# Expert weights stored piece by piece in HBM, an early dummy silu per expert, and result rows added by half rows, in a two-layer trunk kernel

## What is computed

```python
def expert_block(args):
    xb, e = args
    return (jax.nn.silu(xb @ w_gate[e]) * (xb @ w_up[e])) @ w_down[e]
...
y = ys[dest] * g_sorted[:, None].astype(h.dtype)
out = jnp.zeros((T, D), h.dtype).at[tok_sorted].add(y)
```

## Time and profile before

| | us |
|---|---|
| median of three runs | 1378.86 |
| the profiled execution | 1379.58 |
| its span in the trace | 1377.8 |
| PE busy | 1349.4 |
| DVE busy | 1111.5 |
| ACT busy | 920.1 |

### The profile page before, as it was taken

How to read it: one execution, slowest core, us unless ns; L and a number is a source line. 1 busy time by engine, 2 the same in 40 slices (tenths; PEclk the granted TensorE clock), 3 DMA queues, 4 the chain that set the end, 5 groups by cost and what they waited for, 6 DMA issues and landing times.

```text
span 1377.8 us, 17441 instructions
## 1 busy us (share of the span) xinstructions
PE 1349.4 (98%) x6369; PEld 1120.4 (81%) x6369; DVE 1111.5 (81%) x811; ACT 920.1 (67%) x747; POOL 33.8 (2%) x48
## 2 busy tenths in 40 slices
PE   9999999999999999999999999999999999999997
PEld 7888888787877887888788788888878888888775
DVE  5756666655678888888988888898888889889987
ACT  6554444445647777777777777777777777777674
POOL 0000000000110000000000000000000000002000
PEclk9999999999989999999999999999999999999999
DMA  9666775462339999999999999999999999999992
GB/s 347 218 206 181 216 214 191 163 204 92 113 125 372 374 378 362 394 372 364 392 372 370 369 391 372 370 383 366 384 367 392 369 368 388 373 377 381 394 362 93
DMA packets 194940, 431.27 MB, mean 313 GB/s; under 512 B 19601, under 2 KB 22033, under 8 KB 194897
## 3 DMA queue, kind: packets, MB, share of 16 engines
q1 hardware_dynamic: 178752, 415.66, 82.8%
q0 software_dynamic: 3360, 11.78, 2.2%
q10 hardware_dynamic: 12784, 3.26, 1.7%
HBM read 424.89 MB, written 5.78 MB: 313 GB/s over the span
## 4 chain that ended last, share of the span: by engine, by line
PE 89%; DVE 5%; ACT 3%; issue 2%; DMA 0%; ACTq 0%; POOL 0%; DVEq 0%
PE bank_G L1248 10%; PE bank_G L1250 10%; PE bank_G L1249 10%; PE bank_U L1248 9%; PE bank_U L1250 9%; PE bank_U L1249 9%; PE bank_Y L1248 8%; PE bank_Y L1250 8%; PE bank_Y L1249 8%; DVE w_lo L752 2%; PE bank_T L1689 2%; ACT w_hi L454 1%; PE bank_T L1248 1%; PE bank_T L1250 1%; PE bank_T L1249 1%
## 5 line engine op out<-in xcount | busy, mean ns | idle before, releaser
L752 DVE TENSOR_TENSOR w_lo<-raw,w_hi 128x2048 fp32r<-128x2048 f32 x390 | 885.8, 2289 | 195.2 <-ACT w_hi L454 195.1
L454 ACT ACTIVATE w_hi<-raw 128x2048 fp32r<-128x2048 f32 x390 | 747.0, 1919 | 286.7 <-PE bank_U L1250 91.1
L1248 PE MATMUL bank_Y<-w_hi,hidT_hi 128*128 128x512 f32 x492 | 192.3, 391 | 0.0
L1250 PE MATMUL bank_Y<-w_hi,hidT_lo 128*128 128x512 f32 x492 | 191.6, 390 | 0.0
L1249 PE MATMUL bank_Y<-w_lo,hidT_hi 128*128 128x512 f32 x492 | 191.5, 389 | 0.0
L1248 PE MATMUL bank_G<-w_hi,xg_hi 128*128 128x512 f32 x448 | 175.6, 392 | 11.0 <-DVE w_lo L752 10.0
L1248 PE MATMUL bank_U<-w_hi,xg_hi 128*128 128x512 f32 x448 | 179.1, 400 | 0.0
L1250 PE MATMUL bank_U<-w_hi,xg_lo 128*128 128x512 f32 x448 | 175.0, 391 | 0.0
L1250 PE MATMUL bank_G<-w_hi,xg_lo 128*128 128x512 f32 x448 | 174.5, 390 | 0.0
L1249 PE MATMUL bank_U<-w_lo,xg_hi 128*128 128x512 f32 x448 | 174.5, 390 | 0.0
L1249 PE MATMUL bank_G<-w_lo,xg_hi 128*128 128x512 f32 x448 | 174.4, 389 | 0.0
(11 more groups left out here) (302 smaller groups left out, 1366.6 us busy)
## 6 DMA issues: line engine op xcount, KB each, us to landing
raw<-in_expert_w_gate SPq DMA_DIRECT2D x112, 1024.0 KB, 7.4
raw<-in_expert_w_up SPq DMA_DIRECT2D x112, 1024.0 KB, 7.5
raw<-in_expert_w_down SPq DMA_DIRECT2D x112, 1024.0 KB, 7.4
raw<-in_nat_w_qkv SPq DMA_DIRECT2D x12, 1024.0 KB, 5.1
raw<-in_ffn_w_gate SPq DMA_DIRECT2D x11, 1024.0 KB, 8.9
raw<-in_ffn_w_up SPq DMA_DIRECT2D x11, 1024.0 KB, 6.0
raw<-in_ffn_w_down SPq DMA_DIRECT2D x11, 1024.0 KB, 5.1
raw<-in_fourier_w_out SPq DMA_DIRECT2D x4, 1024.0 KB, 15.9
```

The lines of the kernel that those rows point to most:

```text
L454: nc.scalar.activation(w_hi[w][:], raw[s][:], ACT.Copy).then_inc(hi_made, 1)
L752: nc.vector.tensor_tensor(w_lo[w][:], raw[s][:], w_hi[w][:].bitcast(f32), ALU.subtract).then_inc(lo_made, 1)
L1248: nc.tensor.matmul(out_, xh, wh, start=start, stop=False)
L1250: return nc.tensor.matmul(out_, xl, wh, start=False, stop=stop)
```

## The change

Three things. The experts' weights are rearranged on the host into an array of 336 pieces of 128 x 2048, so that each partition of a piece is one run of 8192 bytes. On ACT every expert begins with a silu of one column (which nothing reads), and the splitting of piece 3 goes from the end of the expert before to entry 0 of its own expert, on ACT and DVE. The adding of fetched rows is cut into eight instructions of 128 x 512 in place of four of 128 x 1024, two in each of four steps. (In the second sweep, which is not entered, waits and splits are moved to match.)

```diff
-def expert_source(ewg, ewu, ewd, e, j):
-
-    kind, c, half = EXPERT[j]
-    v = {"gate": ewg, "up": ewu, "down": ewd}[kind][0].rearrange("e (k p) n -> p (e k) n", p=P)
-    if kind == "down":
-        return v[:, bass.ds(e * (FFE // P) + (BANK // P * c + KROW * half), KROW), :], KROW, D
-    return v[:, bass.ds(e * KD + KH * half, KH), BANK * c:BANK * (c + 1)], KH, BANK
+def expert_source(expert_w, e, j):
+
+    return expert_w[bass.ds(e * PER_EXPERT + j, 1)].rearrange("a p n -> p (a n)"), 1, PIECE
...
         def expert(E, ahead, kept=True):
 
+            nc.scalar.activation(mo["silu_first"][:], half_power[:, 0:1], ACT.Silu)
             for j, (kind, c, half) in enumerate(EXPERT):
-                if j < AHEAD - SPLIT:
-                    continue
...
                 if ahead or j + SPLIT < PER_EXPERT:
                     split_hi(j + SPLIT, E)
-            if ahead:
-                for j in range(PER_EXPERT + SPLIT, PER_EXPERT + AHEAD):
-                    split_hi(j, E)
 
         gather_hi(1)
         assert made[0] == N1
-        for j in range(SPLIT, AHEAD):
-            split_hi(j, 0)
...
-        def add_terms(n):
-
-            for b in range(NB):
-                dve.wait_ge(s_terms, 16 * 2 * NB)
-                if n:
-                    dve.wait_ge(terms_added, b + 1)
-                nc.vector.scalar_tensor_tensor(out=h[:, b], in0=mo[("hn_hi", "hn_lo")[n]][:, b].bitcast(f32),
-                                               scalar=mo[("g1", "g2")[n]][:, b:b + 1], in1=h[:, b],
-                                               op0=ALU.mult, op1=ALU.add).then_inc(terms_added, 1)
+        def add_term(n, b, q):
+
+            cs = slice(BANK * q, BANK * (q + 1))
+            dve.wait_ge(s_terms, 16 * 2 * NB)
+            if n:
+                dve.wait_ge(terms_added, 2 * b + q + 1)
+            nc.vector.scalar_tensor_tensor(out=h[:, b, cs], in0=mo[("hn_hi", "hn_lo")[n]][:, b, cs].bitcast(f32),
+                                           scalar=mo[("g1", "g2")[n]][:, b:b + 1], in1=h[:, b, cs],
+                                           op0=ALU.mult, op1=ALU.add).then_inc(terms_added, 1)
...
-                    elif c == 2:
-                        add_terms(0)
-                    elif c == 3:
-                        add_terms(1)
+                    elif 2 <= c < 6:
+                        add_term((c - 2) // 2, c % 2, 0)
...
+                if (kind, half) == ("down", 0) and kept and not sweep and 1 <= c < 5:
+                    add_term((c - 1) // 2, (c - 1) % 2, 1)
...
+def laid_out(w, k0, tiles, c0, width):
+
+    return w.reshape(-1, P, w.shape[-1])[k0:k0 + tiles, :, c0:c0 + width].transpose(1, 0, 2).reshape(P, PIECE)
+
+
+def experts_by_piece(inputs):
+
+    laid = np.empty((NE * PER_EXPERT, P, PIECE), np.float32)
+    for e in range(NE):
+        for j, (kind, c, half) in enumerate(EXPERT):
+            w = np.asarray(inputs[f"expert_w_{kind}"][0][e])
+            place = (BANK // P * c + KROW * half, KROW, 0, D) if kind == "down" else (KH * half, KH, BANK * c, BANK)
+            laid[PER_EXPERT * e + j] = laid_out(w, *place)
+    return laid
```

More of the change, by code:

```diff
@@ L114 @@
 NO_RESULT = (NE - 1) * P
-def expert_source(ewg, ewu, ewd, e, j):
-    kind, c, half = EXPERT[j]
-    v = {"gate": ewg, "up": ewu, "down": ewd}[kind][0].rearrange("e (k p) n -> p (e k) n", p=P)
-    if kind == "down":
-        return v[:, bass.ds(e * (FFE // P) + (BANK // P * c + KROW * half), KROW), :], KROW, D
-    return v[:, bass.ds(e * KD + KH * half, KH), BANK * c:BANK * (c + 1)], KH, BANK
+def expert_source(expert_w, e, j):
+    return expert_w[bass.ds(e * PER_EXPERT + j, 1)].rearrange("a p n -> p (a n)"), 1, PIECE
 def trunk(nc, x, norm_mix, norm_ffn, w_in, w_out, w_qkv, w_o, ffg, ffu, ffd, router_w, router_b,
-          ewg, ewu, ewd, final_norm, gains_c, slide_c, dft_c, mask_c, ident_c, before_c, count_c, out):
+          final_norm, expert_w, gains_c, slide_c, dft_c, mask_c, ident_c, before_c, count_c, out):
     f32, f32r, bf16, i32, u32 = mybir.dt.float32, mybir.dt.float32r, mybir.dt.bfloat16, mybir.dt.int32, mybir.dt.uint32
@@ L134, in trunk @@
     N0 = len(dense)
-    dense += [expert_source(ewg, ewu, ewd, 0, j) for j in range(SPLIT)]
+    dense += [expert_source(expert_w, 0, j) for j in range(SPLIT)]
     N1 = len(dense)
@@ L202, in trunk @@
     arena_start = nc.sbuf_base
-    mo_more = [("y_row", [P, D], f32), ("place", [P, 2, NB], f32), ("past", [P, 2, NB], f32), ("source", [P, 2, NB], u32)]
+    mo_more = [("y_row", [P, D], f32), ("place", [P, 2, NB], f32), ("past", [P, 2, NB], f32), ("source", [P, 2, NB], u32), ("silu_first", [P, 1], f32)]
     moe_l += mo_more
@@ L360, in own_loads @@
             for j in range(AHEAD, PER_EXPERT):
-                src, tiles, _ = expert_source(ewg, ewu, ewd, E % NE, j)
+                src, tiles, _ = expert_source(expert_w, E % NE, j)
                 load(j, E, src, tiles)
@@ L366, in next_loads @@
             for j in range(PER_EXPERT, PER_EXPERT + AHEAD):
-                src, tiles, _ = expert_source(ewg, ewu, ewd, (E + 1) % NE, j % PER_EXPERT)
+                src, tiles, _ = expert_source(expert_w, (E + 1) % NE, j % PER_EXPERT)
                 load(j, E, src, tiles)
         for j in range(SPLIT, AHEAD):
-            src, tiles, _ = expert_source(ewg, ewu, ewd, 0, j)
+            src, tiles, _ = expert_source(expert_w, 0, j)
             load(j, 0, src, tiles)
@@ L726, in _ @@
             act.wait_ge(hn_made, NB)
-            act.wait_ge(terms_added, 2 * NB)
+            act.wait_ge(terms_added, 4 * NB)
             for b in range(NB):
@@ L730, in _ @@
             gather_hi(NE + 1)
-            for j in range(PER_EXPERT, PER_EXPERT + AHEAD):
+            for j in range(PER_EXPERT, PER_EXPERT + SPLIT):
                 split_hi(j, LAST)
@@ L734, in _ @@
                 expert(E, True)
+            split_hi(PER_EXPERT + SPLIT, SECOND[1] - 1)
             act.wait_ge(e_added, NB * (NE + 1))
@@ L1110, in add_result @@
             for b in range(NB):
-                dve.wait_ge(terms_added, NB + b + 1)
+                dve.wait_ge(terms_added, 4 * NB)
                 for q in range(2):
@@ L1785 @@
 _INS = ["x", "norm_mix", "norm_ffn", "fourier_w_in", "fourier_w_out", "nat_w_qkv", "nat_w_o",
-        "ffn_w_gate", "ffn_w_up", "ffn_w_down", "router_w", "router_b", "expert_w_gate", "expert_w_up",
-        "expert_w_down", "final_norm"]
+        "ffn_w_gate", "ffn_w_up", "ffn_w_down", "router_w", "router_b", "final_norm"]
 _OUTS = [((1, S, D), "float32")]
@@ L1818 @@
     gains = np.stack([inputs["norm_mix"], inputs["norm_ffn"]], 1).reshape(4, KD, P).transpose(2, 0, 1)
-    for name, a in [(n, inputs[n]) for n in _INS] + [("gains", gains), ("slide", slide)] + list(shape_constants().items()):
+    for name, a in [(n, inputs[n]) for n in _INS] + [("expert", experts_by_piece(inputs)), ("gains", gains), ("slide", slide)] + list(shape_constants().items()):
         a = np.ascontiguousarray(a)
```

## The result

The changed kernel takes 1368.84 us (median of four runs, 1367.73 to 1369.60) against 1378.80 before: a ratio of 0.9928, 95% interval 0.9911 to 0.9945. The forecast was 1368.0 us, range 1366.8 to 1372.0.

The account below looks back on a forecast made before the run. PE, busy 98% of the span, bounds the kernel, so only its stalls can yield time. Profiled 1379.58 - 8.3 (silu) + 0.3 (piece 3) - 2.9 (half rows), layout 0, = 1368.7; 0.72 above median, so 1368.0 us, range 1366.8 to 1372.0.

Parts of the forecast that it names:

- Silu's table early: Experts 0 to 6: loading silu's table before piece 3's copy removes PE's wait at piece 4, 8.3 us gained.
- Rival 3: ACT in the loop: compiler keeps a load ahead of the real silu too, fourteen loads, 1376.3 us or more; chance 0.03.
- Piece 3 on DVE: Expert 7: result_places comes ahead of piece 3's split on DVE, so PE starts late, 0.3 us lost.
- Half rows: Expert 7, steps 2 to 5: adding by halves cuts PE's stalls of 3.7 us to 0.8, 2.9 us gained.
- rival 2: Expert 7's additions: half rows bring nothing, the eight together stalling as long as the four did, 1370.9 us; chance 0.10.
- The layout: Expert weight transfers: already hidden, so the longer runs are worth 0 on the path.
- rival 4: Weight transfers: 8192-byte runs move slower and become the bound; at 360 GB/s about +43 us, 1422 us; chance 0.04.
- The sum: Whole kernel: profiled 1379.58 - 8.3 + 0.3 - 2.9 = 1368.7, hence 1368.0 us for the median.

Follow-up runs that it names:

- second series: The changed kernel timed once more, unaltered, beside the kernel before and other follow-up kernels: 1367.78 us.
- spread kernel: Changed kernel with each half-row addition ahead of another split and six operations of gate_weights cut into three and three: 1366.85 us; with the old weight layout 1366.12 us.

## Why the prediction was right, and where it was not

- **Silu's table early**, 8.3 us: measured 8.6 alone, and 8.1 to 8.4 by the traces. The steps held to a tenth: the copy of piece 3 is 0.63 late (it starts 3.35 us after that of piece 2, where it was 2.72) for a forecast of 0.62, and 0.35 us are spare for a forecast of 0.33. PE stalls at no piece of the loop. Rival 3 fell: there are seven loads and not fourteen.
- **Piece 3 on DVE**, -0.3 us: this step was wrong, and so are two statements of the section on the change (that the splitting moves on ACT and DVE, and that DVE's `expert` loses the same lines as ACT's). The diff changes ACT alone; DVE had always taken piece 3 at the end of the expert before, and still does, which gives the same order of splits. The term is 0. The kernel that does move it lost 0.25 us, so the price was right for a change that wasn't made.
- **Half rows**, 2.9 us: 3.5 alone (interval 1.9 to 4.4) and 2.8 by the trace. Steps 2 to 5 take 16.9 to 17.0 us each against 16.8 undisturbed: the 0.2 forecast for each, so rival 2 fell. Where the 0.2 goes was partly luck. The prediction had the first half just fit and put all of it at the second gate piece. In the trace most of it is at the first: PE is due at 1280.22, starts at 1280.24 and then restarts slowly, so that the second gate piece starts at 1283.09, 2.85 us later in place of 2.72; the second piece adds about 0.08.

```profile
1279.99 0.39 PE L1241 MATMUL bank_Y<-w_hi,hidT_lo 128*128 128x512 f32 x1
1280.24 0.47 PE L1239 MATMUL bank_G<-w_hi,xg_hi 128*128 128x512 f32 x1
```

A start 0.02 us late costs 0.15 here, and one 0.13 late cost 0.25 when piece 3 was moved on DVE: most of the price of so small a stall is the restart.

- **The layout**, 0: right for the path, since faster transfers meet no one who waits for them; rival 4 fell the other way, with 421 GB/s in place of 402. Missed was the 0.5 to 0.6 us at the end, where the last store lands later; it has nothing to do with the runs.
- **The sum.** The trace's two middle parts give -11.2, the end +0.5, hence -10.7; the medians gave -10.0 and, in the second series, -10.3. That the forecast came within 0.9 us of the median owes something to luck: 0.3 us for a move that wasn't made stood where 0.5 at the end was missing. The 0.4 to 0.7 us that are left were not pinned down, but they are no more than the scatter of a stretch that the prediction took as fixed, the one ahead of the experts. At the router PE runs out of work, and the granted clock goes from 1.00 to 0.50, the lower of its two levels, for a time that changes from profile to profile. Windows of the kernel before:

```profile
385.00:390.00 5.00, 3.59 (x29) 3.15 (x27) 4.49 (x13) 3.41 (x10) 0.45 (x2) 0.91 0.52 211
390.00:395.00 5.00, 5.00 (x24) 5.00 (x25) 3.40 (x13) 2.35 (x3) 1.35 (x2) 0.50 0.00 0
395.00:400.00 5.00, 4.19 (x19) 3.31 (x19) 3.01 (x15) 0.20 (x1) 0.00 (x0) 0.50 0.01 2
400.00:405.00 5.00, 3.93 (x19) 3.24 (x18) 2.50 (x5) 1.08 (x2) 0.00 (x0) 0.73 0.00 0
```

and of the changed kernel's second profile:

```profile
385.00:390.00 5.00, 3.62 (x28) 3.17 (x26) 4.53 (x13) 3.41 (x10) 0.25 (x2) 0.95 0.55 213
390.00:395.00 5.00, 4.94 (x23) 4.94 (x24) 3.38 (x12) 2.54 (x4) 1.55 (x2) 0.50 0.00 0
395.00:400.00 5.00, 3.67 (x22) 2.97 (x22) 3.31 (x17) 0.20 (x1) 0.00 (x0) 0.87 0.00 2
400.00:405.00 5.00, 4.10 (x24) 3.23 (x24) 4.10 (x7) 2.68 (x4) 0.00 (x0) 1.00 0.00 0
```

In the first the clock is at 0.50 up to 400 us, in the second it is back between 395 and 400, and `xg_lo` starts at 404.00 and 402.18. Among all profiles it lies between 402.1 and 404.3, with no relation to the layout (403.2 on average with one large tensor and without), and two profiles of the changed kernel are 0.57 apart. Runs of one program show the same link: of the third series' fifteen runs of the kernel before, the ten with a mean granted clock of 0.993 have spans of 1377.5 us on average, the two with 0.995 of 1375.6. Those fifteen runs spread over 3.1 us in all, and a median of five still carries a part of that.

## What to carry to other kernels

Read a stall back to the engine that made it late, and look for the nearest idle time of that engine: a fixed cost like a table load can go there whole if it and what it pushes stay under the spare time of the next deadline, and here that could be worked out from one trace to a tenth of a microsecond. In a loop, the compiler loads a table ahead of the first activation of the body, so make that one the function that needs it. Where the times of two medians are closer than the runs' scatter, compare the profiles between landmarks that the edit encloses. Small operations of an engine that feeds the bottleneck belong one by one ahead of the pieces with most time to spare, not together ahead of the piece with least; and faster transfers bring nothing where nobody waits for them.

## What the runs showed that was not expected

- Runs of 8192 bytes in place of 2048 and 4096 cut the packets by half and raised what the queues move under load from 402 to 421 GB/s, while landings of undisturbed loads changed little (7.5 to 7.7 us before, 7.0 with the long runs).
- One input tensor of 352 MB in place of three of 117 MB delays the last store's landing from 2.1 to 2.7 us, with either run length.
- A plain copy as the first activation of a hardware loop's body gets a table load of its own (1.28 us).
- The clock's low stretch at the router differs in length from profile to profile, and expert 0's `xg_lo` starts between 402.1 and 404.3 us with it (0.57 us apart in two profiles of the same kernel).
- The lowest times are those of the spread kernel with the old layout, 1366.12 us (ratio to before 0.9912, 0.9899 to 0.9926), and with long runs in three tensors, 1366.74 (0.9911, 0.9898 to 0.9925); the two can't be told apart.
